# Turning the hidden squares of a gated block: sixteen small VectorE transposes against one wide one and sixteen SBUF-to-SBUF transfers

## The reference

```
g, u = split(norm(x) @ w_gate_up)      # 1024 -> 2 x 2816
x   += scale * (silu(g) * u) @ w_down  # 2816 -> 1024
```

## Time and profile before

| | |
|---|---|
| median of 3 runs | 1882.7 us (1882.63 to 1883.42) |
| the profiled execution | 1883.3 us; its span is 1882.0 us, 1.3 us lie outside it |
| PE busy | 1873.4 us, 8974 matmuls |
| DVE busy | 1574.0 us |
| ACT busy | 1103.4 us |
| granted TensorE clock | 1.000 over the span |

### The profile page before, as it was taken

The page is one execution under the profiler, slowest core; times in us unless marked ns, Lnnn a source line. Parts: engine busy times, 40 slices in busy tenths (PEclk is TensorE's granted clock), DMA queues, the critical chain, the costliest instruction groups (busy, mean ns, idle before and its releaser), DMA issues.

```text
span 1882.0 us, 25018 instructions
## 1 busy us (share of the span) xinstructions
PE 1873.4 (100%) x8974; PEld 1572.4 (84%) x8974; DVE 1574.0 (84%) x3072; ACT 1103.4 (59%) x1812; POOL 153.5 (8%) x193
## 2 busy tenths in 40 slices
PE   9999999999999999999999999999999999999999
PEld 7888998888888898888888888888888888888887
DVE  7998789988898868998799878689879987858986
ACT  6554876555655586655555557555555555656553
POOL 1120030000000013000000014100000000500000
PEclk9999999999999999999999999999999999999999
DMA  6765535665666553665466645356655664535653
GB/s 247 238 220 180 197 128 188 217 199 168 199 229 213 168 191 124 201 205 198 160 214 213 204 144 186 113 182 201 201 165 192 212 202 152 180 113 193 206 193 111
DMA packets 97787, 350.25 MB, mean 186 GB/s; under 512 B 10880, under 2 KB 12032, under 8 KB 97408
## 3 DMA queue, kind: packets, MB, share of 16 engines
q1 hardware_dynamic: 95184, 340.13, 54.6%
q10 hardware_dynamic: 2448, 8.53, 1.3%
q0 software_dynamic: 32, 0.00, 0.0%
HBM read 347.57 MB, written 1.05 MB: 185 GB/s over the span
## 4 chain that ended last, share of the span: by engine, by line
PE 94%; DVE 3%; ACT 1%; issue 1%; DMA 0%; SPq 0%; POOL 0%; DVEq 0%; ACTq 0%
PE ps_gu L482 18%; PE ps_gu L480 18%; PE ps_gu L481 18%; PE ps_acc L480 10%; PE ps_acc L482 10%; PE ps_acc L481 10%; PE ps_gu L726 1%; PE ps_gu L727 1%; PE ps_gu L728 1%; PE ps_acc L500 1%; DVE sb_wl L1932 1%; PE ps_gu L1074 0%; DMA sb_scratch<-stream 0%; PE ps_acc L1035 0%; PE ps_tr L480 0%
## 5 line engine op out<-in xcount | busy, mean ns | idle before, releaser
L480 PE MATMUL ps_gu<-sb_wh,sb_xh 128*128 128x512 f32 (+2 forms) x1592 | 620.4, 390 | 0.3 <-DVE sb_wl L1929 0.3
L482 PE MATMUL ps_gu<-sb_wh,sb_xl 128*128 128x512 f32 (+2 forms) x1592 | 617.2, 388 | 0.0
L481 PE MATMUL ps_gu<-sb_wl,sb_xh 128*128 128x512 f32 (+2 forms) x1592 | 616.7, 387 | 0.0
L1257 ACT ACTIVATE sb_wh<-sb_raw,sb_const 128x512 fp32r<-128x512 f32 x344 | 248.2, 721 | 274.6 <-DMA sb_raw<-stream 130.2
L1994 DVE STREAM_TRANSPOSE sb_scratch<-sb_scratch 32x128 f32<-32x128 f32 x1280 | 387.4, 303 | 24.8
L1932 DVE TENSOR_TENSOR sb_wl<-sb_raw,sb_wh 128x1024 fp32r<-128x1024 f32 (+2 forms) x296 | 352.5, 1223 | 23.2 <-ACT sb_wh L1261 20.7
L482 PEld LDWEIGHTS ps_gu<-sb_wh,sb_xl 128*128 128x128 f32 x1592 | 298.9, 188 | 60.0
L480 PEld LDWEIGHTS ps_gu<-sb_wh,sb_xh 128*128 128x128 f32 x1592 | 299.0, 188 | 59.7 <-issue 1.3
L481 PEld LDWEIGHTS ps_gu<-sb_wl,sb_xh 128*128 128x128 f32 x1592 | 299.1, 188 | 58.6
L1261 ACT ACTIVATE sb_wh<-sb_raw 128x1024 fp32r<-128x1024 f32 (+2 forms) x296 | 302.4, 1044 | 64.7 <-DMA sb_raw<-stream 29.6
L1927 DVE SCALAR_TENSOR_TENSOR sb_wl<-sb_raw,sb_const,sb_wh 128x512 fp32r<-128x512 f32 x344 | 257.6, 749 | 90.4 <-ACT sb_wh L1258 90.1
(11 more groups left out here) (279 smaller groups left out, 1580.2 us busy)
## 6 DMA issues: line engine op xcount, KB each, us to landing
sb_raw<-stream SPq DMA_DIRECT2D x620, 512.0 KB, 4.4
sb_raw<-stream SPq DMA_DIRECT2D x8, 416.0 KB, 4.1
sb_raw<-stream SPq DMA_DIRECT2D x8, 390.0 KB, 3.7
sb_scratch<-stream SPq DMA_DIRECT2D x6, 512.0 KB, 8.6
sb_gpost<-post_gains ACTq DMA_DIRECT2D x6, 512.0 KB, 5.2
sb_params<-params ACTq DMA_DIRECT2D x2, 1128.5 KB, 7.7
sb_scratch<-gain_rows ACTq DMA_DIRECT2D x4, 512.0 KB, 5.9
sb_raw<-stream SPq DMA_DIRECT2D x4, 384.0 KB, 3.1
```

What stands on the lines that cost most here:

```text
L480: pe.matmul(out, xh, wh, start=start, stop=False)
L481: pe.matmul(out, xh, wl, start=False, stop=False)
L482: return pe.matmul(out, xl, wh, start=False, stop=stop)
L1257: go(m.wh[:, u % RING, 0:512], m.unit(u)[:, 0:512], ACT.Copy, scale=m.gpre[:, e, k:k + 1])
```

## The change

VectorE turns the 16 x 4 squares of a chunk in place of their partition group with one instruction of 128 x 512 that writes a new tile `m.squares`. SyncE then copies 16 pieces of 32 partitions x 512 bytes (16 KB each) from `m.squares` to `m.hid_t`, each to the partition group where it belongs. These copies stand in SyncE's list ahead of the load of unit 6j+12 of the block, behind a wait for the transposes and for the both_low of the chunk before. both_high waits for the sixteen copies (on one of two semaphores that take turns) instead of the transposes; turn_squares waits for the copies of the chunk before. both_high and both_low read `m.hid_t` and address `m.hh` and `m.hl` in runs of 32 columns, since the order of the blocks in `m.hid_t` is another.

```diff
+    def squares_moved(self, n):
+        return self.moved[n % 2], 256 * ((n + 1) // 2)
...
-        self.hid_t = self.carve(3584, 2, CW)
+        self.squares = self.carve(3072, 4, 4, 32)
+        self.hid_t = self.carve(3584, 4, 4, 32)
+        self.turned_hid = self.hid_t.rearrange("p i b n -> p b i n")
...
+def turn_after_split(f, j):
+    return FIRST_UNIT[FFN_STAGE[f]] + 8 + 6 * j
+
+def by_square(a):
+    return a.rearrange("p t (c i n) -> p (t c) i n", c=2, i=4)
...
     def both_high(f, j):
-        act.wait_ge(*s.squared.at(squared_count(f, j)))
-        go(m.hh[:, both_places(j), :], m.hid_t, ACT.Copy).then_inc(*s.both_high.up())
+        act.wait_ge(*s.squares_moved(squared_count(f, j)))
+        go(by_square(m.hh[:, both_places(j), :]), m.turned_hid, ACT.Copy).then_inc(*s.both_high.up())
...
         for t in range(2):
             vec.wait_ge(*s.hid_done[t].at(11 * f + j + 1))
-        for units in range(4):
-            for tokens in range(4):
-                v = vec.transpose(square(m.hid_t, units, tokens), square(m.hid, tokens, units))
-        v.then_inc(*s.squared.up())
+        n = squared_count(f, j)
+        if n > 1:
+            vec.wait_ge(*s.squares_moved(n - 1))
+        vec.transpose(m.squares.rearrange("p j b n -> p b j n"), m.hid.rearrange("p t (c j n) -> p (t c) j n", c=2, j=4)).then_inc(
+            *s.squared.up())
...
-        tt(m.hl[:, places, :], m.hid_t, m.hh[:, places, :].bitcast(F32), ALU.subtract).then_inc(*s.both_low.up())
+        tt(by_square(m.hl[:, places, :]), m.turned_hid, by_square(m.hh[:, places, :]).bitcast(F32), ALU.subtract).then_inc(
+            *s.both_low.up())
...
+    def move_squares(f, j):
+        n = squared_count(f, j)
+        sp.wait_ge(*s.squared.at(n))
+        if n > 1:
+            sp.wait_ge(*s.both_low.at(n - 1))
+        for i in range(4):
+            for to in range(4):
+                sp.dma_start(m.hid_t[quarter(to), i], m.squares[quarter(i), to]).then_inc(s.moved[n % 2], 16)
+
+    moves = {turn_after_split(f, j) + RAW: (f, j) for f in range(len(FFN_STAGE)) for j in range(LAST)}
...
+        if u in moves:
+            move_squares(*moves[u])
         if u >= EARLY + RAW:
             sp.wait_ge(*s.low_done.at(u - RAW + 1))
         load(u)
+    move_squares(LAST_FFN, LAST - 1)
```

More of the change, by code:

```diff
@@ L236, in __init__ @@
         self.squared = Signal(nc, "hidden_squares_turned")
+        self.moved = [nc.alloc_semaphore(f"hidden_squares_moved_{k}") for k in two]
         self.both_high = Signal(nc, "hidden_high_both")
@@ L439, in both_places, with quarter @@
     return slice(2 * (j % 2), 2 * (j % 2) + 2)
-def square(a, of_partitions, of_columns):
-    blocks = a.rearrange("p t (i n) -> p (t i) n", i=2)
-    return blocks[32 * of_partitions:32 * of_partitions + 32, :, 32 * of_columns:32 * of_columns + 32]
+def quarter(i):
+    return slice(32 * i, 32 * i + 32)
+def turn_after_split(f, j):
+    return FIRST_UNIT[FFN_STAGE[f]] + 8 + 6 * j
+def by_square(a):
+    return a.rearrange("p t (c i n) -> p (t c) i n", c=2, i=4)
 def by_head(a, n):
@@ L1988, in turn_squares @@
     def turn_squares(f, j):
+        assert at_unit[0] == turn_after_split(f, j), (f, j, at_unit[0])
         for t in range(2):
             vec.wait_ge(*s.hid_done[t].at(11 * f + j + 1))
-        for units in range(4):
-            for tokens in range(4):
-                v = vec.transpose(square(m.hid_t, units, tokens), square(m.hid, tokens, units))
-        v.then_inc(*s.squared.up())
+        n = squared_count(f, j)
[3 more added lines that the diff above has]
+            *s.squared.up())
     def both_low(f, j):
```

## The result

| | before | after |
|---|---|---|
| median | 1882.94 us (4 runs, 1882.63 to 1883.42) | 2198.18 us (4 runs, 2194.19 to 2200.14) |
| ratio | | 1.1671, 95% interval 1.1651 to 1.1691 |
| span of the profiled execution | 1882.0 us | 2198.8 us |

The change makes the kernel 315 us slower, six times what was forecast, and outside the range. The page of the changed kernel answers to the earlier trace rows, and its first waits of PE to the earlier trace rows. Columns as there.

A forecast was written before the change was run, and what follows sets the result against it. PE was taken as the bound. Over eight blocks, stalls of 12.0 us (chunk 0), 10.3 (chunk 1), nothing (chunks 2 to 8) and 30.1 (chunk 9) made 52.4 us, on the median 1882.7 giving 1935; range 1886 to 1985.

The forecast's parts named there:

- what bounds the kernel: PE, busy 1873.4 of 1882.0 us; work taken from VectorE can give back at most PE's idle 8.6 us.
- the wide transpose: On VectorE, one 128 x 512 transpose replaces sixteen and takes 0.71 us, with ends 0.6 and 1.21.
- the issue of a copy: On SyncE, each of sixteen back-to-back issues takes 0.46 us, range 0.37 to 0.47; the last goes out 6.9 us after the first.
- chunks 2 to 8 at nothing: In each block these chunks add no time, as a turn takes 16.28 us and PE needs 16.32.
- B: Time from the first copy's issue to the last copy's landing: 8.5 us, with ends 7.05 and 9.25.
- the landing: The last 16 KB copy lands 1.6 us after its issue, range 1.5 to 2.2.
- From S to the down product: From the start of turn_squares to PE's down product: 10.69 us, before 8.10 where nothing else held it.
- S to S: From one start of turn_squares on VectorE to the next: 16.28 us, 17.61 for chunk 0.
- Chunk 9: Its down follows chunk 8's after only 12.24 us, so it loses 3.76 us per block, 30.1 over eight blocks.
- Cheap issues: Rival: an issue on SyncE costs 0.37 to 0.41 us and a landing 1.5, giving 1884 to 1891 us; chance 0.27.
- The loads as the bound: Rival: loads queued behind the copies land after 4.3 us, giving 1981 us; chance 0.16, shared with slow landing or doubled both_high/both_low.
- A gain: Rival: issues under 0.29 us let the down product start earlier, giving 1879 us; chance 0.05, 0.03 by more than 0.2%.

The follow-up runs named there:

- no_copies: Changed kernel without any copies, both_high and both_low waiting for the wide transpose alone and reading its output: 1882.12 us, ratio 0.9995 to the kernel before.
- p128: Changed kernel with each of the sixteen copies made 128 partitions x 128 bytes instead of 32 x 512 bytes, SBUF to SBUF: 2219.9 us (one run).
- from_hbm: Changed kernel with the sixteen copies of 32 partitions x 512 bytes reading the weight stream in HBM instead of the squares: 1990.84 us (one run).
- load_first: Changed kernel with the copies one place later in SyncE's list, behind the load of unit 6j+12: 2302.8 us (one run).

## Why the prediction was wrong, step by step

**Right: what bounds the kernel.** PE was the chain, and VectorE's time is worth nothing (no_copies). VectorE's busy time fell by 323 us and not by 347: the 4.3 us a chunk came from first start to last end of the sixteen transposes, with the gaps between them, which are not busy time.

**Right: the wide transpose.** 0.71 us forecast, 0.71 measured. The views in runs of 32 columns cost nothing: both_high takes 0.63 and both_low 0.69, as before.

**Wrong: the issue of a copy.** This is the step that failed first. "I take 0.46: the back-to-back row is the nearer situation", with 0.47 as the upper end. It is 0.63, so the sixteen take 9.43 us from first to last and not 6.9. The row was of loads from HBM, and I treated the number of partitions as the only difference; p128 and from_hbm show that it makes none, and that both ends in SBUF, to which I gave no thought, make the 0.17. The upper end should have been well above the nearest row, since no row showed a copy from SBUF to SBUF. It was not even the upper end of the rows: two rows further on in the same timeline of SyncE stand the six loads at 5.43 that follow each other every 0.64 us.

**Wrong: chunks 2 to 8 at nothing.** This step failed too. from_hbm is nearly the forecast's own case, issues 0.46 apart and a landing of 1.64, B 8.58 against 8.5. It measured 1990.84 (one run) where the forecast had 1935 and the range ended at 1985. So the right price for an issue would not have saved the forecast; what was missing is worked out below.

**Nearly right: the landing.** 1.6 forecast, 1.8 measured, within 1.5 to 2.2. The 2.0 us that the Trainium skill (DMA: Bandwidth & Descriptors, section on the anatomy of one DMA) gives as the fixed part lies about as far on the other side; the section gives it for transfers issued by GpSimd, and these are issued by SyncE. Its rule for kernel authors that transfers under 64 KB are mostly overhead and should be merged is borne out: one copy of 256 KB costs nothing here and sixteen of 16 KB cost 315 us. But the overhead that counts is the issuing engine's, 16 x 0.63 in a row, and not the fixed part of each transfer, which overlaps.

**Right: the form of both paths.** With the measured 0.63 and 1.8, B is 9.43 + 1.80 = 11.23. "From S to the down product" is then 2.19 + 11.23 = 13.42; measured 13.38 in the turn above, and 13.46 in the first chunk of the kernel (37.18 - 23.72). "S to S" is 7.78 + 11.23 = 19.01; measured 18.99 in the turn above. But it is a floor and not a mean: over chunks 1 to 8 of all blocks the mean is 19.45.

```profile
23.72 0.71 DVE L2011 STREAM_TRANSPOSE sb_scratch<-sb_scratch 128x512 f32<-128x512 f32 x1
...
37.18 0.80 PE L495 MATMUL ps_acc<-sb_wh,sb_fr 128*128 128x512 f32 x1 [5.62 <-DVE sb_fr L2017]
```

**The sum, with the term corrected.** Chunk 0: 8 x 13.42 - 73.5 = 33.9. Chunk 1: (20.34 - 16.32) x 8 = 32.2. Chunks 2 to 8: (19.01 - 16.32) x 56 = 150.6, where 0 was forecast. Chunk 9: (19.01 - 12.24) x 8 = 54.2. Together 271, of 317 in the span. The same sum for from_hbm, with B = 6.94 + 1.64 = 8.58, is 59, and it measured 108. The table sets both beside what the traces give, part by part (the starts of down and of the transposes, compared with those of the kernel before):

| us over eight blocks | by the sum | changed kernel | by the sum | from_hbm |
|---|---|---|---|---|
| chunk 0 | 33.9 | 34.9 | 12.7 | 15.1 |
| chunk 1 | 32.2 | 32.6 | 11.0 | 12.5 |
| chunks 2 to 8 | 150.6 | 176.6 | 2.2 | 32.5 |
| chunk 9 | 54.2 | 55.5 | 33.0 | 32.8 |
| after down of chunk 9 | 0 | 17.7 | 0 | 14.7 |
| all | 271 | 317 | 59 | 108 |

**Missing: about 46 us, in two places.** *Chunks 2 to 8*, 26 us here and 30 in from_hbm. The forecast took every turn to last the same. At PE's pace a shorter turn wins next to nothing and a longer one costs in full, so that scatter alone costs time. The rows of the kernel before had shown it: its turns that do not yet wait for PE take 14.9 to 16.0 us, and the 15.0 of the prediction is one of the shortest. Two sources of it can be read from the trace. Issues do not all take the same time: sixteen take 9.43 us from first to last start in most chunks, but one of them can take up to 1.7 us (the maximum above), and over the 80 chunks this adds 18 us. 32 issues take over 0.65 us, and 24 of these lie within half a microsecond of a 16 KB packet on the queue that the profile calls instruction; none of that queue's packets falls into a burst without such an issue beside it. I take these for waits for instructions; no run tested it, and whose instructions they are is not shown (the queue moves 71 such packets in both kernels). And in 31 of the 64 turns it is the load behind the copies that ends last and not the copies (its landing + 4.6 against the start of both_high + 7.0), by 11 us in all.

*After the down product of chunk 9*, where PE is the chain again, a block takes longer than before by 1.4 to 2.8 us beyond the stall of the next chunk 0, 17.7 us in all. There PE restarts at half clock. The 8 us behind the stall of chunk 9, in the first and in the eighth block:

```profile
214.18:222.18 8.00, 8.00 (x30) 6.48 (x31) 3.79 (x6) 3.03 (x8) 0.00 (x0) 0.82 0.63 219
...
2177.43:2185.43 8.00, 8.00 (x24) 6.33 (x25) 2.74 (x4) 0.91 (x3) 0.00 (x0) 0.65 0.00 0
```

A granted clock of 0.82 over 8 us is 8 x 0.18 = 1.4 us lost, and the first block is 1.41 longer; in the eighth it is 8 x 0.35 = 2.8, and 2.76 longer. In each of the eight blocks the two agree within 0.2 us, and PE stands idle there no longer than in the kernel before. So the clock accounts for this part, a cost of a stall that the prediction ("a stall of PE is not given back") had not in its sum. Inside a block the half clock costs nothing, as S to S does not go through gate_up there.

A slip in the prediction's working changes little: with B at 8.1 seven turns win 0.44 each, so chunk 9 would cost 4.5 us and not 8.

**The rivals.** Cheap issues: refuted, the lone 0.33 was no guide to a burst. The loads as the bound: not alone the bound (load_first), but level with the copies, where I had called their cost hidden. The load behind the copies lands 3.6 us after its issue (median), not 2.8. With the forecast's own issues this path would already have been 8.1 + 3.6 + 4.6 = 16.3, as long as that of the copies. A gain: refuted even without any copy.

## What to carry to other kernels

A small transfer costs its issuing engine a time that did not depend on its size here (0.59 us for 16 and for 32 KB in a burst from SBUF to SBUF, 0.42 for 16 KB from HBM), and in a chain a burst of them adds up one by one while bytes and landings overlap: count the issues before the bytes, and ask what waits in the same list behind them. Price a burst from the slowest burst in the trace, not from the first row that looks alike. Where a new loop comes out within a few per cent of the bound engine's pace, the forecast is a cliff and not a number: state what the next 0.1 us of each unshown term would cost, widen the end on that side, and count the scatter of the turns as a cost, since a late turn is lost and an early one wins nothing. Before work is taken off an engine, look for waits of the bound engine that end on it; here there was 0.3 us, and 325 us less work on VectorE gave nothing.

## What was not expected of the hardware

- Back-to-back issues from SyncE start 0.63 us apart from SBUF to SBUF and 0.46 with the source in HBM. From SBUF to SBUF it is 0.63 for 32 partitions and 0.64 for 128. Issued alone, a copy of 128 x 2 KB takes 0.47 us from SBUF to SBUF and 0.34 from SBUF to HBM.
- SyncE and ScalarE issue such bursts at the same time, 8 and 8 in 4.95 and 5.28 us, and SyncE is no slower by it.
- The stall of PE of 2.33 us before 1193.60 is followed by some 3.1 us at a granted clock of 0.51. Not every such stall is: after 2.88 us before 1051.02 the clock stayed at 1.00, and so it did after six others of 2.3 to 2.7 us in the same trace. Over the changed kernel the half clock adds 110 us to PE's busy time, and 17.7 us of this lengthen the kernel where PE is the chain.
